# Scan stage of a hybrid encoder: inverse summed in its PSUM bank, with the early columns of two matrices as one operand

## The chip, the core and the metric

The kernel runs on one core of one Trainium2 chip. The metric is the device time of one execution in microseconds (us), as the median of several runs. TensorE (PE) multiplies matrices and writes to PSUM (eight banks of 512 float32 columns on 128 partitions), VectorE (DVE) and ScalarE (ACT) read and write both memories, GpSimd (POOL) works on SBUF, SyncE (SP) issues most of the transfers. The engines run side by side and wait for each other on semaphores; each works off its own instructions in order. All data is float32.

## What is computed

One layer: a projection feeds three mixers (gMLP, bidirectional RWKV-7, bidirectional mLSTM), their outputs are concatenated and projected, normed, and go through a mixture of 32 experts. The change is in the RWKV-7 scan. Cut from the reference:

```python
def _wkv7_step(state, inp):
    r, w, k, v, a, b = inp
    sa = jnp.einsum('phvk,phk->phv', state, a)
    state = state * w[:, :, None, :] + sa[..., None] * b[:, :, None, :] + v[..., None] * k[:, :, None, :]
    return state, jnp.einsum('phvk,phk->phv', state, r)
...
    _, out = lax.scan(_wkv7_step, state0, xs)      # 256 steps, 2 directions, 6 heads of 64
    out = _merge_dirs(...)
    out = _head_norm(out, RWKV_GN_EPS).reshape(bn, sn, R_WIDTH) * ln_g + ln_b
```

A chunk of 128 steps is done at once: with strictly triangular M (products of the vectors a and b within the chunk) the step-by-step correction is the inverse of a unit triangular 128x128 matrix. The mLSTM and expert parts are:

```python
    sc = jnp.einsum('phtd,phsd->phts', qc, kc) * jnp.exp(dmat - m_t[..., None])
...
    return ((u_ + 1.0) * (g_ * jax.nn.sigmoid(g_ * SWIGLU_ALPHA))) @ w2[e] + b2[e]
```

## The kernel before

The program is written engine by engine, each with its instructions in a fixed, hand-written order. It has three stages in time: the input projection with its preparations (to about 117 us), the scan stage (117 to 294 us), and output projection, norm, routing and experts (to the end). SP loads the experts' weights, 403 MB in all, in 2 MB loads; two of the first expert loads are issued inside the scan stage, three (L511) when the last scan output is done, and the rest follows as slots come free.

The scan stage goes over three pairs of heads (`for pt in range(NP)`), and in each pair over 2 directions d x 2 chunks x 2 heads, so that each direction has four 128x128 matrices side by side in one PSUM bank. Per pair:

- **Products.** PE multiplies keys with queries and keys with keys (L1024, contraction over 64 rows); DVE evicts each bank of 512 columns with a triangular mask (L1608) into `nqT` and `mpT`.
- **Start of the inverse.** POOL adds the identity to M (L1335) and masks off all but 2x2 blocks (L1338), giving `xmT`. PE transposes that (L1037), ACT copies it to `xm` (L733). PE also turns keys (L1032, L1033), evicted by ACT (L730).
- **Levels** m = 2, 4, 8, 16, 32, 64: the inverse of the 2m blocks comes from that of the m blocks X: PE forms M X (L1045), DVE masks the product to the blocks between an early and a late group (L1613, into `gm`), PE forms the new X (L1058, bank 4d+1) and its transpose (L1059, bank 4d+2), ACT evicts both (L738, L739). All at full width, four matrices per direction.
- **Solution, state and output.** PE and ACT work through W, U and the state in two steps over the chunks (L1087 to L1122), then ACT copies the output (L774).

Other work is woven in between the levels by hand. On PE: gate columns and bonus sums (L990, L1005), m rows (L958) and scores (L966) of the mLSTM heads, their weighing (L980), the turning of the former pair's scans (L997). On DVE after the two masks of a level: at m=2 gate rows (first pair) or `scans_out` and the first half of a norm (L1582, L1376 to L1381), and the decay scan of the next pair (L1457); at m=4 the decay arguments (L1551), the second half of the norm (L1387, L1595 to L1600), `prep_relative`; at m=8 the weights (L1561), another norm, `prep_keys`; at m=16 a norm's end, decay arguments, the division; at m=32 weights; at m=64 division and `prep_operands` (L1487 to L1492), whose end lets the next pair's products start. On ACT: roots of the norms (L691, L694), the exponentials of the factors (L725) and of the decays (L705 to L708). On POOL: the masking of the factors (L1327).

## Time and profile before

| | |
|---|---|
| median of 3 runs | 1267.39 us (1267.28 to 1267.82) |
| the profiled execution | 1271.03 us, span 1269.1 us |
| mean granted clock of TensorE | 0.993 |
| busy in the span | PE 1199.1, DVE 303.2, ACT 218.6, POOL 34.1 us |
| read from memory | 428.44 MB |
| scan stage | 117.0 to 293.7 us |

Busy times are sums over records of one engine, and a record that overlaps the next is not counted twice. A record's "idle before" is the time its engine stood still ahead of it, and the arrow names whose work ended that. PEclk is the granted clock of TensorE as a share of full speed (2.4 GHz; 0.5 is 1.2 GHz). In the chain of waits each line is a piece of the path that ended last, with start and length. A float32 matmul leaves two records each of weight load and of matmul, a transpose one. Line numbers are those of the kernel before, unless said otherwise.

### The profile page before, as it was taken

To read this page: it belongs to the slowest core of one execution; us is meant where nothing else is said; L and a number is where in the kernel's file an instruction comes from. 1 tells how busy PE (TensorE), PEld (TensorE's weight loads), DVE (VectorE), ACT (ScalarE), POOL (GpSimd) and SP (SyncE) were. 2 spreads that over 40 slices of the span, in tenths; PEclk is the share of its full clock that TensorE was granted. 3 is DMA by queue.
4 is the path that set the end of the run, shared out by engine and by line. 5 is a ranking of instruction groups with operands and counts; after the bars stand their busy time and mean duration, and the time that the engine had idled before them with its cause. 6 is when DMAs were issued, how large, how long until landed. Compare 5 with 4: busy or idle time off the path is not lost.

```text
span 1269.1 us, 15346 instructions
## 1 busy us (share of the span) xinstructions
PE 1199.1 (94%) x6265; PEld 552.5 (44%) x6265; DVE 303.2 (24%) x751; ACT 218.6 (17%) x432; POOL 34.1 (3%) x44
## 2 busy tenths in 40 slices
PE   7999999999999999999999999999999999999996
PEld 6874889795433333333333333333333333333332
DVE  1344757454511111111111111111111111111113
ACT  2233334232111111111111111111111111111112
POOL 1001020110000000000000000000000000000001
PEclk9999999999999999999999999999999999999998
DMA  9324000117999999997999999999999999999994
GB/s 334 146 88 164 1 1 1 70 69 278 371 401 429 429 428 429 428 428 301 429 430 429 428 429 429 429 427 429 429 428 429 429 428 427 430 428 429 428 428 184
DMA packets 41599, 429.89 MB, mean 339 GB/s; under 512 B 3756, under 2 KB 8851, under 8 KB 16739
## 3 DMA queue, kind: packets, MB, share of 16 engines
q1 hardware_dynamic: 39616, 426.29, 80.3%
q0 software_dynamic: 688, 2.06, 0.5%
q10 hardware_dynamic: 1267, 1.15, 0.4%
q8 instruction: 20, 0.33, 0.1%
q14 instruction: 8, 0.07, 0.0%
HBM read 428.44 MB, written 1.05 MB: 338 GB/s over the span
## 4 chain that ended last, share of the span: by engine, by line
PE 67%; DMA 21%; DVE 6%; ACT 2%; POOL 1%; issue 1%; SPq 1%; ACTq 0%; POOLq 0%; DVEq 0%
PE bank L1252 24%; DMA pool<-in_exp_w 19%; PE bank L1284 14%; PE bank L886 5%; PE bank L1226 3%; PE bank L896 3%; PE bank L1045 2%; PE bank L1059 2%; PE bank L1236 2%; PE bank L1058 2%; PE bank L1271 2%; DVE pool L1803 1%; DVE pool L1798 1%; DVE pool L1800 1%; ACT pool L823 1%
## 5 line engine op out<-in xcount | busy, mean ns | idle before, releaser
L1252 PE MATMUL bank<-pool 128*64 128x512 f32 x1024 | 230.8, 596 | 6.1 <-DMA pool<-in_exp_w 6.1
L1252 PE MATMUL bank<-ring,pool 128*64 128x512 f32 x1024 | 230.9, 596 | 5.8 <-DMA ring<-in_exp_w 5.8
L1284 PE MATMUL bank<-ring,pool 128*64 128x512 f32 x1024 | 226.8, 595 | 0.0
L1284 PEld LDWEIGHTS bank<-ring,pool 128*64 128x64 f32 x1024 | 70.7, 137 | 153.9 <-issue 153.9
L1252 PEld LDWEIGHTS bank<-pool 128*64 128x64 f32 x1024 | 70.1, 137 | 150.7 <-issue 139.1
L1252 PEld LDWEIGHTS bank<-ring,pool 128*64 128x64 f32 x1024 | 70.0, 137 | 150.7 <-issue 137.2
L1784 DVE TENSOR_SCALAR pool<-pool 128x128 f32<-128x128 f32 x64 | 19.3, 346 | 420.6 <-PE bank L1252 420.6
L1796 DVE TENSOR_SCALAR pool<-bank 128x512 f32<-128x512 f32 x32 | 22.2, 693 | 331.7 <-PE bank L1252 331.7
L1226 PE MATMUL bank<-pool 64*128 64x512 f32 x264 | 65.6, 614 | 0.7 <-ACT pool L827 0.7
L1212 PE MATMUL bank<-pool 128*64 128x512 f32 x264 | 62.3, 593 | 1.0 <-DVE pool L1757 1.0
L827 ACT ACTIVATE pool<-bank 128x512 f32<-128x512 f32 x32 | 19.1, 598 | 250.5 <-PE bank L1284 250.5
L886 PE MATMUL bank<-pool,ring 128*128 128x256 f32 x272 | 61.2, 387 | 0.0
L817 ACT ACTIVATE pool<-bank 128x256 f32<-128x256 f32 x32 | 12.3, 385 | 279.4 <-PE bank L1264 279.4
L886 PEld LDWEIGHTS bank<-pool,ring 128*128 128x128 f32 x272 | 52.6, 194 | 7.7 <-issue 0.3
L819 ACT ACTIVATE pool<-pool 128x512 f32<-128x512 f32 x32 | 20.2, 632 | 195.5 <-DVE pool L1796 195.5
L1059 PE MATMUL bank<-ring 128*128 128x128 f32 x288 | 53.5, 280 | 0.0
L1058 PE MATMUL bank<-ring 128*128 128x128 f32 x240 | 48.8, 286 | 0.5 <-DVE ring L1613 0.5
L1236 PE MATMUL bank<-pool 32*64 32x512 f32 x392 | 36.4, 610 | 9.6 <-ACT pool L823 9.6
L1059 PEld LDWEIGHTS bank<-ring 128*128 128x128 f32 x288 | 43.0, 196 | 0.2
L1226 PEld LDWEIGHTS bank<-pool 64*128 64x128 f32 x264 | 22.6, 185 | 43.2 <-issue 41.6
L1045 PE MATMUL bank<-ring 128*128 128x128 f32 x288 | 38.1, 285 | 0.8 <-ACT ring L739 0.8
L1058 PEld LDWEIGHTS bank<-ring 128*128 128x128 f32 x240 | 37.3, 196 | 2.7 <-DVE ring L1613 1.7
(295 smaller groups left out, 938.9 us busy)
## 6 DMA issues: line engine op xcount, KB each, us to landing
ring<-in_exp_w SPq DMA_DIRECT2D x127, 2048.0 KB, 20.6
pool<-in_exp_w SPq DMA_DIRECT2D x64, 2048.0 KB, 27.4
ring<-in_w_in SPq DMA_DIRECT2D x4, 2048.0 KB, 9.2
ring<-in_w_out SPq DMA_DIRECT2D x2, 2048.0 KB, 7.9
ring<-in_w_in SPq DMA_DIRECT2D x2, 1536.0 KB, 13.7
ring<-in_exp_w SPq DMA_DIRECT2D x2, 1024.0 KB, 22.3
ring<-in_w_in SPq DMA_DIRECT2D x1, 1632.0 KB, 6.4
pool<-in_consts SPq DMA_DIRECT2D x1, 1601.0 KB, 19.5
```

What stands on the lines that cost most here:

```text
L886: last = mm(bank[i % 4][:, 0:S], w[:, k, col:col + P], xT[:, k], start=(k == 0), stop=(k == KD - 1))
L896: last = mm(bank[(NT + j) % 4][:, 0:n], xT[:, k, P * c:P * c + P], w[:, k, :], start=(k == 0), stop=(k == KD - 1))
L1045: last = mm(pview(4 * d, 0, 4, P)[:, j], mpT[:, d, j, 0:P], xm[:, d, j], start=True, stop=True)
L1058: mm(pview(1 + 4 * d, 0, 4, P)[:, j], xmT[:, d, j], gm[:, d, j], start=True, stop=True)
L1059: last = mm(pview(2 + 4 * d, 0, 4, P)[:, j], gm[:, d, j], xmT[:, d, j], start=True, stop=True)
L1212: last = mm(bank[7][SLOTS * hf:SLOTS * hf + SLOTS, :], sel[:, c], x_tok[:, c, 512 * hf:512 * hf + 512], start=(c == 0), stop=(c == NCH - 1))
L1226: last = mm(bank[2 * c + hf][:, :], gT[hp, P * c:P * c + P], ysb[hp, :], start=False, stop=stop, skip_group_check=True)
L1236: last = mm(bank[4 + g][SLOTS * hf:SLOTS * hf + SLOTS, :], esel[gp], bias[gp, 512 * hf:512 * hf + 512], start=True, stop=False)
L1252: last = mm(bank[4 + g][hp, :], lhs, w[:, k % 2, o:o + 512], start=False, stop=(k == KD - 1))
L1271: last = tr(pview(4, 0, 4, P)[:, j], hr[:, j:j + 509:4], ident)
L1284: last = mm(bank[6][SLOTS * hf:SLOTS * hf + SLOTS, :], hT[:, k % 4, SLOTS * (k // 4):SLOTS * (k // 4) + SLOTS], w2s[k // 4][:, k % 4, 512 ...
L1796: V.tensor_scalar(hr, bank[4][:, :], 7.0, None, ALU.min).then_inc(s_hg, 1)
```

## The change

The levels are m = 1, 2, 4, ..., 64 now, and a level works on half the columns. Only blocks between an early group of m columns and the late group behind it change in a level. So `early_columns` (POOL) copies the early columns of M of two matrices into one 128-column operand, ACT evicts from the inverse only the late and the early columns of the next level (`y_late`, `y_early`), `cross` (PE) multiplies them, `turn_early` transposes the early columns, and `update` adds into the inverse Y, which stays in its PSUM bank (4d+1) from an identity matmul at m=1 to the end (start=False); it writes every other group of m columns there. POOL's two steps at the start of a pair, the full-width transposes and the separate transpose of X are gone. The product of b and a is formed in both orders by matmuls of 128 columns, and the key products come behind them (bank 3 and 4d+2), on PE and DVE, beside level m=1. The woven work stands at the same m as before, behind the masks of DVE. W is written to bank 4d instead of 4d+1. Constants shrink from 3202 to 2818 columns, in the same space.

```diff
-LEVELS = (2, 4, 8, 16, 32, 64)
+LEVELS = (1, 2, 4, 8, 16, 32, 64)
...
+        mp = rview(2, 2048, 2, 2, 4, P)
+        m_early = [view(o_xT + 512 * b, 2, 2, P) for b in range(4)]
+        ym = rview(3, 0, 2, 4, P)
+        tT = rview(3, 1024, 2, 2, P)
+        gm = rview(3, 2048, 2, 2, P)
...
+        def part(a, n, late):
+            return a.rearrange("p j (b two m) -> p two (j b) m", two=2, m=LEVELS[n])[:, late]
...
# ACT
+                for n in range(NL):
                     for d in range(2):
-                        if n < len(LEVELS) - 1:
-                            A(xm[:, d], pview(1 + 4 * d, 0, 4, P), ACT.Copy)
-                        A(xmT[:, d], pview(2 + 4 * d, 0, 4, P), ACT.Copy).then_inc(s_xup, 1)
+                        if n:
+                            act.wait_ge(s_tt, 12 * pt + 2 * n + d - 1)
+                            A(tT[:, d], pview(4 * d + 2, 0, 2, P), ACT.Copy).then_inc(s_tev, 1)
...
+                        if n < NL - 1:
+                            A(half_cols(y_late(d), n + 1), part(y, n + 1, 1 - d), ACT.Copy).then_inc(s_xup, 1)
+                            A(half_cols(y_early(d), n + 1), part(y, n + 1, d), ACT.Copy).then_inc(s_yup, 1)
+                        else:
+                            A(ym[:, d], y, ACT.Copy).then_inc(s_xup, 1)
...
# PE
+                def cross(n, d):
...
+                    for jj in range(2):
+                        if n:
+                            early, late = m_early[(n - 1) % 4][:, d, jj], y_late(d)[:, 2 * jj:2 * jj + 2]
+                        else:
+                            early = mp[:, d, 1, 2 * jj:2 * jj + 2].rearrange("p j s -> p (j s)")[:, d:d + 255:2]
+                            late = ident[:, 1 - d:P:2].unsqueeze(1).broadcast_to([P, 2, HD])
+                        last = mm(pview(4 * d, 0, 2, P)[:, jj], early, late, start=True, stop=True)
...
+                def update(n, d):
...
+                    for jj in range(2):
+                        lhs = tT[:, d, jj] if n else scan_const(C_T1 + P * d, P)
+                        last = mm(part(pview(4 * d + 1, 2 * P * jj, 2, P), n, 1 - d), lhs, gm[:, d, jj], start=False,
+                                  stop=(n == NL - 1), skip_group_check=True)
...
-                        for j in range(4):
-                            last = mm(pview(4 * d, 0, 4, P)[:, j], mpT[:, d, j, 0:P], xm[:, d, j], start=True, stop=True)
...
-                        for j in range(4):
-                            if n < len(LEVELS) - 1:
-                                mm(pview(1 + 4 * d, 0, 4, P)[:, j], xmT[:, d, j], gm[:, d, j], start=True, stop=True)
-                            last = mm(pview(2 + 4 * d, 0, 4, P)[:, j], gm[:, d, j], xmT[:, d, j], start=True, stop=True)
...
# POOL
-                    nc.gpsimd.tensor_tensor(m, m, ident.unsqueeze(1).broadcast_to([P, 4, P]), ALU.add).then_inc(s_pch, 1)
-                    pool.wait_ge(s_pch, 2 * pt + d + 1)
-                    x2 = scan_const(C_X2 + P * d, P)
-                    nc.gpsimd.tensor_tensor(xmT[:, d], m, x2.unsqueeze(1).broadcast_to([P, 4, P]), ALU.mult).then_inc(s_gps, 1)
+                for n in range(1, 5):
+                    early_columns(pt, n)
                 mask_factors(2 * pt)
+                for n in range(5, NL):
+                    early_columns(pt, n)
                 mask_factors(2 * pt + 1)
...
# DVE
-                        V.tensor_tensor(gm[:, d], pview(4 * d, 0, 4, P), wide(gmask(d, n), 4), ALU.mult).then_inc(s_g, 1)
+                    V.tensor_tensor(gm[:, d], pview(4 * d, 0, 2, P), wide(gmask(n), 2), ALU.mult).then_inc(s_g, 1)
```

**PE, level m=4 of the first pair.** First the kernel before, from the product of direction 0 to the first update of direction 1:

```order
L1045 MATMUL bank0<-ring 128x128 [waits x_evacuated]
L1045 MATMUL bank0<-ring 128x128 x3
L1045 MATMUL bank4<-ring 128x128 [waits x_evacuated]
L1045 MATMUL bank4<-ring 128x128 x3
L990 MATMUL bank7<-pool 128x6 [waits gate_rows_ready]
L990 MATMUL bank7<-pool 128x6 x7
L1005 MATMUL bank7<-pool 128x2 [waits bonus_products_ready]
L1005 MATMUL bank7<-pool 128x2
L958 MATMUL bank3<-ring,pool 128x256 x2
L1058 MATMUL bank1<-ring 128x128 [waits level_product_masked]
L1059 MATMUL bank2<-ring 128x128
```

The same place after the change, direction 1 of the cross products (L1083) and the transposes (L1090) up to the updates (L1100), with the changed kernel's line numbers:

```order
L1083 MATMUL bank4<-ring,pool 128x128 [waits early_columns_of_operand_ready]
L1083 MATMUL bank4<-ring,pool 128x128
L1090 MATMUL bank6<-pool,ring 128x128 [waits early_columns_of_inverse_evacuated]
L1090 MATMUL bank6<-pool,ring 128x128
L1020 MATMUL bank7<-pool 128x6 [waits gate_rows_ready]
L1020 MATMUL bank7<-pool 128x6 x7
L1035 MATMUL bank7<-pool 128x2 [waits bonus_products_ready]
L1035 MATMUL bank7<-pool 128x2
L988 MATMUL bank3<-ring,pool 128x256 [waits key_products_evacuated]
L988 MATMUL bank3<-ring,pool 128x256
L1100 MATMUL bank1<-ring 128x32x4 [waits early_columns_evacuated,level_product_masked]
L1100 MATMUL bank1<-ring 128x32x4
```

Two products and two updates stand where four and eight stood for a direction, and the update, which goes to pieces of 4 columns, waits for ACT's copy of the transposes as well as for DVE's mask.

**DVE, start of the second pair.** Before, the last four of the eight evictions and the first masks:

```order
L1608 TENSOR_TENSOR ring<-bank2,pool 128x512 [waits products_done]
L1608 TENSOR_TENSOR ring<-bank0,pool 128x512 [waits products_done]
L1608 TENSOR_TENSOR ring<-bank6,pool 128x512 [waits products_done]
L1608 TENSOR_TENSOR ring<-bank4,pool 128x512 [waits products_done]
L1613 TENSOR_TENSOR ring<-bank0,pool 128x512 [waits level_product_done]
L1613 TENSOR_TENSOR ring<-bank4,pool 128x512 [waits level_product_done]
L1582 COPY pool<-bank7 128x256 [waits scan_out_turned]
```

After, from the last of four evictions of products (L1699) on: L1693 evicts the key products, L1688 is the mask.

```order
L1699 TENSOR_TENSOR ring<-bank5,pool 128x2x2x128 [waits products_done]
L1693 TENSOR_TENSOR ring<-bank3,pool 128x512 [waits key_products_done]
L1688 TENSOR_TENSOR ring<-bank0,pool 128x256 [waits level_product_done]
L1693 TENSOR_TENSOR ring<-bank2,pool 128x512 [waits key_products_done]
L1688 TENSOR_TENSOR ring<-bank4,pool 128x256 [waits level_product_done]
L1693 TENSOR_TENSOR ring<-bank6,pool 128x512 [waits key_products_done]
L1693 TENSOR_TENSOR ring<-bank3,pool 128x512 [waits key_products_done]
L1688 TENSOR_TENSOR ring<-bank0,pool 128x256 [waits level_product_done]
L1688 TENSOR_TENSOR ring<-bank4,pool 128x256 [waits level_product_done]
L1662 COPY pool<-bank7 128x256 [waits scan_out_turned]
```

The masks of m=1 stand between the evictions of the key products, and the copy of the scans comes behind the masks of m=2, as before.

## Rows read from the trace of the kernel before

**Rows 1.** Busy times by stretch: us, PE, PEld, DVE, ACT, POOL, PEclk, DMA, GB/s.

```profile
117.03:177.46 60.43, 56.52 (x456) 50.58 (x456) 38.56 (x89) 24.31 (x52) 7.85 (x8) 0.97 0.11 36
177.46:234.65 57.19, 54.04 (x451) 48.55 (x451) 37.08 (x93) 22.38 (x51) 7.86 (x8) 1.00 0.09 32
234.65:293.74 59.09, 55.96 (x460) 50.80 (x460) 33.09 (x86) 20.46 (x47) 9.80 (x11) 0.97 0.13 45
```

**Rows 2.** Groups by shape, 119 to 296 us: count | busy us, mean ns | idle before.

```profile
L1059 PE MATMUL bank<-ring 128*128 128x128 f32 x288 | 53.5, 280 | 0.0
L1058 PE MATMUL bank<-ring 128*128 128x128 f32 x240 | 48.8, 286 | 0.5 <-DVE ring L1613 0.5
...
L1045 PE MATMUL bank<-ring 128*128 128x128 f32 x288 | 38.1, 285 | 0.8 <-ACT ring L739 0.8
...
L1327 POOL TENSOR_TENSOR pool<-pool 128x256 f32<-128x256 f32 x12 | 8.5, 727 | 94.9 <-ACT pool L725 94.9
...
L1561 DVE TENSOR_TENSOR pool<-pool,bank 128x256 f32<-128x256 f32 x12 | 5.0, 416 | 2.4 <-POOL pool L1327 2.4
...
L730 ACT ACTIVATE ring<-bank 128x256 f32<-128x256 f32 x6 | 2.3, 383 | 13.3 <-PE bank L1033 13.3
```

**Rows 3.** Chain of waits at the second pair's start: start us, us, what.

```profile
177.53 1.11 PE bank L1024 x8
...
183.93 1.27 POOL ring L1338
...
185.90 1.84 PE bank L1045 x16
```

**Rows 4.** DVE in order of time, second pair: start us, us, what [idle before].

```profile
188.39 0.42 DVE L1582 COPY pool<-bank 128x256 f32<-128x256 f32 x1
...
192.42 0.69 DVE L1613 TENSOR_TENSOR ring<-bank,pool 128x512 f32<-128x512 f32 x1
...
195.19 1.40 DVE L1551 TENSOR_SCALAR pool<-bank,pool 128x256 f32<-128x256 f32 x4 [0.64 <-PE bank L958]
...
201.10 0.69 DVE L1613 TENSOR_TENSOR ring<-bank,pool 128x512 f32<-128x512 f32 x1 [0.20 <-PE bank L1045]
...
209.22 1.52 DVE L1613 TENSOR_TENSOR ring<-bank,pool 128x512 f32<-128x512 f32 x2 [0.53 <-PE bank L1045]
...
216.06 1.52 DVE L1613 TENSOR_TENSOR ring<-bank,pool 128x512 f32<-128x512 f32 x2 [1.24 <-PE bank L1045]
...
222.92 0.69 DVE L1613 TENSOR_TENSOR ring<-bank,pool 128x512 f32<-128x512 f32 x1 [2.88 <-PE bank L1045]
```

**Rows 5.** DVE in order of time, first pair (two rows) and third pair.

```profile
134.04 1.29 DVE L1613 TENSOR_TENSOR ring<-bank,pool 128x512 f32<-128x512 f32 x2
...
151.84 1.29 DVE L1613 TENSOR_TENSOR ring<-bank,pool 128x512 f32<-128x512 f32 x2
...
257.25 0.42 DVE L1600 TENSOR_TENSOR pool<-pool 128x256 f32<-128x256 f32 x1
...
264.14 0.17 DVE L1381 TENSOR_SCALAR pool<-pool 128x4 f32<-128x4 f32 x1
```

**Rows 6.** ACT, then POOL, in order of time around m=16, second pair.

```profile
214.82 0.63 ACT L705 ACTIVATE ring<-ring 128x512 f32<-128x512 f32 x1
...
216.47 0.84 ACT L725 ACTIVATE pool<-pool 128x768 f32<-128x768 f32 x1
...
217.39 1.41 POOL L1327 TENSOR_TENSOR pool<-pool 128x256 f32<-128x256 f32 x2 [15.12 <-ACT pool L725]
```

**Rows 7.** Busy times of two stretches of 4 us, columns as in rows 1.

```profile
136.00:140.00 4.00, 4.00 (x23) 4.00 (x23) 2.60 (x9) 1.08 (x2) 0.00 (x0) 0.57 0.02 4
...
184.00:188.00 4.00, 2.75 (x23) 2.73 (x24) 0.91 (x2) 1.07 (x2) 1.19 (x1) 1.00 0.00 0
```

**Rows 8.** Chain of waits behind the scans; then the busy times of 300 us.

```profile
301.78 14.69 DMA pool<-in_ln_b
...
642.00:942.00 300.00, 291.64 (x1428) 99.44 (x1430) 38.79 (x95) 34.28 (x64) 0.00 (x0) 1.00 1.01 428
```

More of the change, by code:

```diff
@@ L62, in constants @@
         before = (row < col) if d == 0 else (row > col)
[L63 to L72 removed]
+        o = C_MASK2 + 3 * P * d
+        c[:, o:o + P] = before
+        c[:, o + P:o + 2 * P] = before | (row == col)
+        c[:, o + 2 * P:o + 3 * P] = before.T
+        c[:, C_T1 + d * P:C_T1 + d * P + P] = col == 2 * (row % HD) + d
+    for n, m in enumerate(LEVELS):
+        c[:, C_GM + n * P:C_GM + n * P + P] = (row // HD == col // HD) & (row % HD // m == col % HD // m)
     c[:, C_HSEL:C_HSEL + 2] = row // HD == np.arange(2)[None, :]
@@ L331, in encoder_kernel, with wide, rows @@
                "mg": (2 * GW + 2 * RW, RW)}
+        def wide(a, n):
+            return a.unsqueeze(1).broadcast_to([P, n] + list(a.shape[1:]))
+        def rows(key, pt):
+            o = LNO[key][0] + P * pt
+            return wide(lnb[:, o:o + P], 2)
         s_x = sem("x_loaded")
@@ L1016, in _, with key_products @@
                 pe.wait_ge(s_ops, pt + 1)
-                for n in range(0, len(FILLS), 2):
-                    d, f, _ = FILLS[n]
-                    if f == 0:
-                        pe.wait_ge(s_prev, 8 * pt + 1 + 2 * d)
+                for d in range(2):
+                    for c in range(NCH):
+                        for a in (1, 0):
+                            for h in range(2):
+                                hp = slice(HD * h, HD * h + HD)
+                                keys, queries = bt[hp, d, c], ar[hp, d, c, a]
+                                lhs, rhs = (keys, queries) if a else (queries, keys)
+                                o = 256 * c + P * (1 - a)
+                                last = mm(bank[4 * d + h][:, o:o + P], lhs, rhs, start=True, stop=True)
+                                if c == 1 and a == 0:
+                                    last.then_inc(s_prod, 1)
+                def key_products(d):
+                    if d:
+                        pe.wait_ge(s_nqe, 4 * pt + 1)
+                    elif pt:
+                        pe.wait_ge(s_oTe, pt)
                     for c in range(NCH):
@@ L1039, in _ @@
-                for n in range(len(LEVELS)):
+                                last.then_inc(s_nqf, 1)
+                def cross(n, d):
+                    if n:
+                        pe.wait_ge(s_me, 12 * pt + 2 * n + d - 1)
+                    for jj in range(2):
+                        if n:
+                            early, late = m_early[(n - 1) % 4][:, d, jj], y_late(d)[:, 2 * jj:2 * jj + 2]
[3 more added lines that the diff above has]
+                        last = mm(pview(4 * d, 0, 2, P)[:, jj], early, late, start=True, stop=True)
+                    last.then_inc(s_a, 1)
@@ L1040, in _ @@
+                key_products(0)
+                for n in range(NL):
                     for d in range(2):
-                        pe.wait_ge(s_xup, 14 * pt + 2 * n + d + 1)
                         if n == 0:
-                            pe.wait_ge(s_prev, 8 * pt + 6 + 2 * d)
-                        for j in range(4):
-                            last = mm(pview(4 * d, 0, 4, P)[:, j], mpT[:, d, j, 0:P], xm[:, d, j], start=True, stop=True)
-                        last.then_inc(s_a, 1)
-                    if n == 1:
+                            pe.wait_ge(s_prev, 4 * pt + 2 * d + 2)
+                            cross(0, d)
+                            mm(bank[4 * d + 1][:, :], ident, ident.unsqueeze(1).broadcast_to([P, 4, P]), start=True,
+                               stop=False, skip_group_check=True)
+                            continue
+                        pe.wait_ge(s_xup, 2 * NL * pt + 2 * (n - 1) + d + 1)
+                        if n == 1:
+                            pe.wait_ge(s_nqe, 4 * pt + 2 + d)
+                        if n == 2:
+                            tr(pview(4 * d + 2, 0, 4, P)[:, 2], bt[:, d, d], ident)
+                            tr(pview(4 * d + 2, 0, 4, P)[:, 3], kt[:, d, d], ident).then_inc(s_bk, 1)
+                        if n == 3:
+                            pe.wait_ge(s_bkev, 2 * pt + d + 1)
+                        cross(n, d)
+                        turn_early(n, d)
+                    if n == 0:
+                        if pt:
+                            scans_turned(pt - 1)
+                        key_products(1)
+                    if n == 2:
@@ L1314, in _ @@
         def _(pool):
+            psteps = [0]
             nc.gpsimd.memset(hst, 0.0)
@@ L1390, in flat @@
                 return a.rearrange("p c h e -> p (c h) e")
-            def rows(key, pt):
-                o = LNO[key][0] + P * pt
-                return wide(lnb[:, o:o + P], 2)
-            def wide(a, n):
-                return a.unsqueeze(1).broadcast_to([P, n] + list(a.shape[1:]))
             dve.wait_ge(s_ptr, 1)
```

183 lines of the change are left out of this document (98 added, 85 removed).

## The prediction

> **What bounds the kernel now.** I read the stretches of the three head pairs first. From the first product matmul of a pair to that of the next it takes 60.43, 57.19 and 59.09 us, 176.7 us in all, and TensorE (PE) is busy for 56.5, 54.0 and 56.0 of them, VectorE (DVE) for 38.6, 37.1 and 33.1, ScalarE (ACT) for some 22, GpSimd (POOL) for 8 to 10 [rows 1]. So the scan stage is bound by PE, and DVE is the next in line. The groups by shape say what PE does: 816 records of the level loop, L1045, L1058 and L1059 [rows 2]. One 128x128 float32 matmul leaves two records, and in the chain 16 records, 8 matmuls, take 1.84 us [rows 3]: 0.23 us a matmul. A reader on another engine starts about 0.17 us after PE could go on to the next (a record lasts 280 ns but comes every 115).
>
> Then the end of the kernel: behind the scans the expert weights stream in at 428 GB/s with the DMA share at 1.0 [rows 8], and their large loads start when the last scan output is done. The 14.69 us of the norm row behind three of these loads [rows 8] hangs on the same event. So whatever the scans save moves the stream, and with it the end, by as much. I find no cover for it.
>
> **Part 1: PE work removed.** Before, a pair has 48 + 40 + 48 = 136 matmuls of 128 columns in its levels (816/3/2) and eight transposes. Now a level from m=2 on has four products (cross), four updates and four transposes of half price (a transpose leaves one record): 8 x 0.23 + 4 x 0.11 = 2.3 us against 24 x 0.23 = 5.5. Six such levels are 13.7 us, the new level m=1 with its two 512-column identity matmuls (four times 128 columns each, 0.9 us) is 3.6. Sum 17.3 against 136 x 0.23 + 0.9 = 32.2: 15 us of PE work per pair, 45 in all. PE then needs about 40 us per pair. That is no longer far from DVE's 37, and neither engine will be busy all the time, so the sum must be made along the path.
>
> **Part 2: DVE.** The eight evictions of 512 columns per pair stay. Twelve masks of 512 columns at 0.69 us become fourteen of 256. The nearest row for such a mask is L1561, 0.42 us with one operand in PSUM [rows 2]. The norm steps, decay arguments, weights and preparations stay where they were, between the masks, and there they are the bound from now on.
>
> **Part 3: the start of a pair.** Before, DVE's evictions, two POOL steps for each direction (1.27 us each, the last at 183.93), the transposes and an ACT copy stand in series: first product 177.5, first level product 185.9, the first pair of masks done and the next DVE block started at 188.39, 10.9 us in [rows 3, 4]. After: PE's own row is 1.8 (products) + 0.95 (key products) + 2 x (0.45 + 0.9) (cross and identity) + 0.4 (turning the last pair's scans) + 0.95 (other key products) + 0.45 (first update) = 7.3; then 0.17, an ACT copy of 256 columns (L730: 0.38, [rows 2]), a cross of 0.45 and 0.17 again put the first m=2 mask at 8.5, the second 0.7 later, the block at 9.5. POOL's copies of early columns are not in it: priced as L1327, 0.73 us for 128x256 [rows 2], eight of them from 2.5 us on end at 8.5, and level n needs only the n-th two. If such a copy cost 1.3 as the older POOL steps do, the third level's would still be in time.
>
> **Part 4: the levels, worked for the second pair.** Times from its first product, now | then:
> - m=2 block (scan output, norm, decay scan) 188.39 to 192.42 [rows 4]: 4.0 us of pure DVE, unchanged. Masks m=4 at 15.0 | 13.5.
> - m=4: before, DVE waited until 195.19 for the m rows behind 12 updates and products, then worked 5.9 us to the next mask at 201.10. Now the m rows are ready by 13.7; two masks and a copy take 0.9, the rest 5.7. Masks m=8 at 23.6 | 20.1.
> - m=8: 8.12 us now (201.10 to 209.22), PE-bound by little. Two masks at 0.34 plus 6.1 of weights, norm and key preparation: 6.8. Masks m=16 at 31.8 | 26.9.
> - m=16: 6.84 now. Masks and 4.2 of DVE work: 5.0. Masks m=32 at 38.6 | 31.9.
> - m=32: 6.86 now (216.06 to 222.92). Then: the chain here is not DVE. The decay arguments are out at 30.2; ACT copies the m=16 results until 29.3, runs the decay exponentials (1.65, from 214.82 to 216.47) and then the factors (0.84) until 31.7; POOL masks them (1.41) until 33.1 [rows 6], DVE multiplies until 34.4, PE weighs (1.3) until 35.7 and only then issues the cross for m=64, whose mask starts at 36.3 | 45.5 before.
> - m=64 and the tail: the rest of the level is 1.7 us of PE; from the last update to the next pair's first product it is 9.1 now and stays, since its steps only change banks (the last mask starts at 222.92, it and the 16 records of its updates take 2.6, and 225.5 to 234.65 is the 9.1).
> Sum: 36.3 + 1.7 + 9.1 = 47.1 against 57.2, a gain of **10.1**.
>
> **First pair.** Its m=2 block is 2 us longer (gate rows; next masks at 134.04) and the m=8 block 1.1 us longer, ending at 151.84 [rows 5]; the start is 0.4 shorter, and at m=8 the factors' masking on POOL is waited for. The same walk gives 48.0 against 60.4: **12.4**, of which 1.7 is a stretch at half clock that the trace has at 136 to 140 [rows 7].
> **Third pair.** No preparation for a fourth: its blocks end at 257.67 (L1600) and 264.3 (L1381) [rows 5], 1.4, 1.7 and 2.9 us shorter than the second's. Today PE covers that; then it is gained, with PE bound in the last levels. The walk gives 43.5 against 59.1: **15.6**.
> Sum 38.1 us.
>
> **The clock.** In 136 to 140 the granted clock was 0.57, about 1.2 GHz for most of it, and PE worked on [rows 7]; the third pair, at a mean of 0.97 [rows 1], must hold another. In the first pair PE had waited shortly before, for the gate rows. In the new kernel PE waits more often: by my walk some 5 us nearly idle before m=32 in the first two pairs and 2 us at m=4. I allow for two to three such stretches on the path, 1.7 us each: 4 us. The Trainium skill ("TensorE: Matmul & The Clock Gate", What's actually happening) says that the throttled clock is the default and that activity releases it; the trace agrees as far as it goes, and by that rule alone every idle level start would be a candidate.
> Forecast gain 38 - 4 = **34 us**. The profiled execution took 1271.0 us around a span of 1269.1, 3.6 above the median 1267.4 of the runs; it would go to 1237, the median to **1233.4**.
>
> **A rule against the change.** The update writes its result into every other group of m columns of a PSUM bank. No row shows a matmul that does this: all level rows write 128 columns in a row at 0.23 us [rows 2, 3]. Bounds: no extra, or twice the time, as if each column took a second cycle. Doubling adds 0.9 us to each level's PE work; it stays hidden in the DVE-bound levels m=4 to m=16 and shows at m=1, 2, 32 and 64: about 3.5 us per pair, 10 us in all, 1244. The Trainium skill ("SBUF — State Buffer", Door 1: The DMA port swizzle) states that non-contiguous PSUM access significantly slows matmuls; it gives no factor. I take none, since from m=2 on the columns come in runs and only m=1 writes single ones, and keep 10 us for the range.
>
> **Rivals.**
> - *Slow PSUM writes*, as priced: 1240 to 1247. Chance 0.10.
> - *Half clock over much of the scans*: one more us for each us of PE work so run. With a third of the 120 us, two thirds of them on the path less the waits: 15 to 25 us back, 1245 to 1260. For it: the stretches there are. Against: PE at 2.75 busy of 4 us at 184 to 188 kept its full clock there and in the second pair after it [rows 1, 7]. Chance 0.07.
> - *Slower than before*: the same mechanism without end. If nearly all of the new scans' 120 us of PE work ran at 1.2 GHz, 120 comes on top of 139, less some 18 of waits: 240 against 177, 1330. It decides from about 55 us of PE work at half clock. Chance 0.02.
> - *DVE and POOL hold each other up, or the chain through ACT copies is longer than rows show* (nine ACT copies and exponentials per level with two hand-overs each): 2 to 4 us per pair, 1238 to 1245. Chance 0.11.
> - *The gain does not reach the end*, because the weight stream is bound by an earlier start: it would stay at 1267 with DMA waits growing. The DMA share of 0.09 to 0.13 in the scans [rows 1] speaks against it. Chance 0.02.
> - *More than forecast*: no half-clock stretch and overlaps that I put in series: 1222 to 1228. Chance 0.10.
> - The forecast, 1228 to 1240: 0.58.
>
> **How the numbers follow.** Faster by more than 0.2% (2.5 us, about what can be told from no change): all but the fifth and the slower one, 0.95. Same 0.02, slower 0.03. Range: 1224 to 1249, which leaves out the tails of the clock cases and of the better one, near 0.18.
>
> **What would show it.** In the new profile: three pairs of about 47, 48 and 43 us; PE busy near 40 in each; 256-column masks near 0.42; after them no DVE wait at m=8 and m=16; update records as quick as the cross ones (else the PSUM rival); the granted clock by stretch; the time from the last scan output to the end unchanged at 975 us. Wrong if a pair stays above 52 us, or if that last stretch grows.

## The result, and the profile after

| | before | after |
|---|---|---|
| median, runs of one chip | 1267.61 us (1267.28 to 1268.63, 4 runs) | 1250.24 us (1246.84 to 1253.96, 4 runs) |
| ratio | | 0.9862 (95%: 0.9831 to 0.9894) |
| profiled execution | 1271.03 us, span 1269.1 | 1248.53 us, span 1246.7 |
| mean granted clock | 0.993 | 0.979 |

Faster, by 17.4 us instead of the 34 forecast; 1250.2 lies one microsecond outside the range. The kernel after also scatters: its four runs took 1246.84, 1248.53, 1251.96 and 1253.96 us at mean granted clocks of 0.984, 0.979, 0.978 and 0.976, in that order.

The three pairs in the kernel after, as [rows 1] are before (columns: us, then PE, PEld, DVE, ACT and POOL busy, PEclk, DMA share, GB/s):

```profile
115.22:170.79 55.57, 49.03 (x333) 41.02 (x333) 36.10 (x91) 24.24 (x66) 7.07 (x16) 0.82 0.11 39
170.79:223.39 52.60, 46.30 (x328) 38.80 (x327) 35.40 (x95) 22.28 (x65) 8.18 (x16) 0.87 0.09 33
223.39:270.63 47.24, 44.30 (x337) 37.67 (x337) 31.73 (x88) 20.47 (x61) 9.64 (x19) 0.93 0.16 58
```

155.4 us instead of 176.7 before and 138.6 forecast. The records of PE fell from 1367 to 998, but it is busy for 139.6 us and not for the 120 of the forecast, because the granted clock is 0.82, 0.87 and 0.93 where it was 0.97, 1.00 and 0.97 [rows 1]. From the last scan output (270.63) to the end of the span it takes 976.1 us, against 975.4 before: what the scans save arrives at the end, as forecast.

PE in order of time in the second pair, around the update of m=8 (L1100), the weighing (L1010), the m rows (L988) and the cross products of m=16 (L1083):

```profile
187.93 0.71 PE L1083 MATMUL bank<-ring,pool 128*128 128x128 f32 x4
...
189.14 0.38 PE L1090 MATMUL bank<-pool,ring 128*128 128x128 f32 x2
192.75 2.07 PE L1100 MATMUL bank<-ring 128*128 128x128 f32 x8 [3.23 <-DVE ring L1688]
194.62 2.66 PE L1010 MATMUL bank<-pool 128*128 128x65 f32 x12
197.21 2.07 PE L988 MATMUL bank<-ring,pool 6*128 6x256 f32 x4
199.21 1.22 PE L1083 MATMUL bank<-ring,pool 128*128 128x128 f32 x4
```

And the busy times of the stretches of 4 us there:

```profile
188.00:192.00 4.00, 1.52 (x12) 1.28 (x12) 3.83 (x9) 1.41 (x4) 3.82 (x6) 0.97 0.00 0
192.00:196.00 4.00, 3.25 (x15) 3.25 (x16) 3.86 (x12) 1.32 (x4) 0.00 (x0) 0.50 0.00 0
196.00:200.00 4.00, 4.00 (x13) 3.04 (x14) 2.91 (x7) 0.42 (x2) 0.00 (x0) 0.50 0.00 0
200.00:204.00 4.00, 3.27 (x19) 2.91 (x17) 2.61 (x8) 2.00 (x7) 0.00 (x0) 0.75 0.00 0
204.00:208.00 4.00, 3.21 (x12) 2.51 (x13) 2.51 (x11) 2.57 (x7) 1.41 (x2) 0.68 0.00 0
```

PE waits 3.23 us for DVE's m=8 masks, the clock goes to 0.50, that is 1.2 GHz, and the work behind the wait takes 1.7 to 1.8 times as long as the same records do at full clock (in e1_fill below): the update 2.07 us against 1.16, the weighing 2.66 against 1.55, four cross records 1.22 against 0.71. In turn DVE waits for PE, and of the 10.1 us forecast for this pair 4.6 arrive. Over the whole stage such stretches add up to 41 us at half clock; before they were 7. (In every figure of this kind a 4-us window with a granted clock of c counts as 2 x (1 - c) x 4 us at half clock, and the windows are summed.)

### The profile page after: what moved, and what is told of

Same layout as the page of the kernel before. It is cut to its first block, busy times and chain, and to the rows that moved or that the text cites. A ratio compares the mean times of both kernels' runs of the same rounds, so it can differ in the third digit from the quotient of the medians.

```text
span 1246.7 us, 14734 instructions
## 1 busy us (share of the span) xinstructions
PE 1172.2 (94%) x5893; PEld 519.7 (42%) x5893; DVE 297.7 (24%) x757; ACT 218.4 (18%) x474; POOL 33.5 (3%) x68
## 4 chain that ended last, share of the span: by engine, by line
PE 67%; DMA 20%; DVE 7%; ACT 2%; issue 1%; SPq 1%; ACTq 0%; POOL 0%; POOLq 0%; DVEq 0%
PE bank L1326 24%; DMA pool<-in_exp_w 20%; PE bank L1358 15%; PE bank L916 5%; PE bank L1300 3%; PE bank L926 3%; PE bank L1310 2%; PE bank L1211 2%; PE bank L1083 2%; PE bank L1345 2%; DVE pool L1899 1%; DVE pool L1894 1%; PE bank L1100 1%; DVE pool L1896 1%; ACT pool L853 1%
## 5 line engine op out<-in xcount | busy, mean ns | idle before, releaser
L1326 PEld LDWEIGHTS bank<-pool 128*64 128x64 f32 x1024 | 70.3, 137 | 151.0 <-issue 138.4
L1345 PE MATMUL bank<-pool 128*128 128x128 f32 x128 | 24.0, 310 | 15.3 <-DVE pool L1899 15.3
L1345 PEld LDWEIGHTS bank<-pool 128*128 128x128 f32 x128 | 17.9, 209 | 43.4 <-DVE pool L1899 43.4
L926 PE MATMUL bank<-ring,pool 128*128 128x384 f32 (+2 forms) x96 | 35.3, 528 | 0.0
L1286 PEld LDWEIGHTS bank<-pool 128*64 128x64 f32 x264 | 18.9, 137 | 38.2 <-issue 37.1
L1100 PE MATMUL bank<-ring 128*128 128x128 f32 x144 | 27.0, 331 | 6.1 <-DVE ring L1688 5.7
```

The costliest lines, as they stand in the source:

```text
L926: last = mm(bank[(NT + j) % 4][:, 0:n], xT[:, k, P * c:P * c + P], w[:, k, :], start=(k == 0), stop=(k == KD - 1))
L1100: last = mm(part(pview(4 * d + 1, 2 * P * jj, 2, P), n, 1 - d), lhs, gm[:, d, jj], start=False, stop=(n == NL - 1), skip_group_check=True)
L1286: last = mm(bank[7][SLOTS * hf:SLOTS * hf + SLOTS, :], sel[:, c], x_tok[:, c, 512 * hf:512 * hf + 512], start=(c == 0), stop=(c == NCH - 1))
L1326: last = mm(bank[4 + g][hp, :], lhs, w[:, k % 2, o:o + 512], start=False, stop=(k == KD - 1))
L1345: last = tr(pview(4, 0, 4, P)[:, j], hr[:, j:j + 509:4], ident)
```

## Experiments

Theory: PE, with a good quarter less to do (998 records instead of 1367), waits for DVE more often; the clock falls at such waits; the PE work behind them is on the path. Rivals: the path at full clock is simply longer than I walked it (DVE and POOL hold each other up, long hand-overs through ACT), or the updates' strided PSUM writes are slow.

### Filling PE's waits

```diff
+fill_sum(SUM_FILL[pt][n])        # k x mm(bank[1][:, 0:P], zeros, ident, start=False, stop=False)
 for d in range(2):
     update(n, d)
+fill_cross(CROSS_FILL[pt][n])    # k x mm(bank[0][:, 0:P], ident, ident, start=True, stop=True)
+SUM_FILL:   8 ahead of the gate columns; m=8: 8, 12, 5; m=16: 10, 6, 2 (pairs 1, 2, 3)
+CROSS_FILL: m=4: 2, 2, 2; m=16: 6, 6, 7
```

The fillers need a matrix of zeros, so 128 columns of constants are loaded more; the other variants with fillers have them too.

> The changed kernel, with 76 matmuls of 128x128 put into TensorE's waits: 51 of zeros, summed into the inverse's own bank before the updates (no value changes), 25 whose result nobody reads, in the cross bank, before the scores. At 0.23 us each that is 17.5 us of matmuls in places where PE waits 16 to 20 us for VectorE. Theory (the clock falls to 1.2 GHz after the waits, and what PE does next at half speed is on the path): the 4-us stretches of the scans with a granted clock near 0.5, 41 us of them in the changed kernel, go but for a few us; the pairs take 48 to 51, 48 to 50 and 43 to 46 us instead of 55.6, 52.6 and 47.2; the time 1234 to 1239 us, ratio to before 0.974 to 0.978, and the runs lie within 2 us of each other. Rival A (the path at full clock is longer than I walked it: held-up VectorE, long ACT chain): the clock is mended, but the time stays at 1247 to 1252. Rival B (filler work is only more work): 1252 to 1262.

Measured: 1238.72 us (1237.80 to 1239.09), ratio 0.9736 (0.9720 to 0.9752), mean clock 0.995. On this chip before took 1270.53. The three pairs:

```profile
117.29:167.00 49.71, 48.10 (x401) 41.53 (x401) 36.12 (x91) 24.12 (x66) 7.33 (x16) 1.00 0.13 44
167.00:216.00 49.00, 46.52 (x380) 39.61 (x379) 35.39 (x95) 22.07 (x65) 8.20 (x16) 1.00 0.10 37
216.00:262.07 46.07, 44.80 (x369) 38.41 (x369) 31.63 (x88) 20.27 (x61) 9.65 (x19) 1.00 0.17 58
```

No stretch at half clock is left and the pairs take 144.8 us, 10.6 less than in the changed kernel, although PE has 76 matmuls more. The numbers of the theory came in, the narrow scatter too; only the third pair, at 46.07 us, lies a shade above its 43 to 46. Rival B is out, and so is rival A as the whole cause. In part rival A holds: at full clock the pairs still take 6.2 us more than the 138.6 forecast.

The same kernel decides on the PSUM rival, since its clock is 1.00 throughout. Groups by shape of the three pairs (count | busy us, mean ns | idle before); L1086 are the cross products, L1103 the updates:

```profile
L1086 PE MATMUL bank<-ring,pool 128*128 128x128 f32 x144 | 23.3, 285 | 0.1
L1103 PE MATMUL bank<-ring 128*128 128x128 f32 x144 | 22.3, 288 | 1.0 <-DVE ring L1704 1.0
...
L1103 PE MATMUL bank<-ring,pool 128*128 128x128 f32 x24 | 3.5, 288 | 0.0
```

The updates, which write every other group of m columns of a bank, take 288 ns a record, the cross products, which write their columns in a row, 285. The last row is the updates of m=1, where single columns are written: 288 as well. There the chain of waits of the kernel after has four updates in the time of any four products (start us, us, what):

```profile
177.85 1.09 PE bank L1100 x8
```

So for float32 writes of this kind the statement of the Trainium skill that I had kept a range for ("SBUF — State Buffer", Door 1) shows no effect here.

### The same instructions with six columns

```diff
-mm(bank[1][:, 0:P], zeros, ident[:, 0:P], ...)
+mm(bank[1][:, 0:6], zeros, ident[:, 0:6], ...)      (the cross fillers likewise)
```

> As e1_fill with the same 76 instructions in the same places, but each with 6 columns instead of 128, so PE is hardly busier. Theory: that they are there changes nothing; the clock stays at half in the same stretches, 1247 to 1254 us as the changed kernel. Rival (it is the issuing or the order that helps, not the columns): the time follows e1_fill.

Measured: 1256.41 us (1252.62 to 1269.56, 10 runs), ratio 0.9912 (0.9877 to 0.9947). The first two pairs, and then one filler group (24 records, 12 matmuls) at full clock and one of 12 records at half:

```profile
115.89:172.12 56.23, 55.34 (x401) 48.11 (x401) 36.09 (x91) 24.16 (x66) 7.06 (x16) 0.85 0.11 39
172.12:229.40 57.28, 56.20 (x379) 49.25 (x379) 35.37 (x95) 22.27 (x65) 8.17 (x16) 0.79 0.09 31
```

```profile
192.29 2.74 PE L1110 MATMUL bank<-pool 128*128 128x6 f32 x24
...
203.34 2.56 PE L1110 MATMUL bank<-pool 128*128 128x6 f32 x12
```

The clock falls as without fillers (47.8 us at half clock), so their mere presence does nothing. The median lies 2.4 us above the 1247 to 1254 expected, and the runs form two groups, six at 1252.6 to 1256.6 us and four at 1266.1 to 1269.6; why is open. In one thing the expectation was wrong: PE is not "hardly busier". A 6-column matmul with 128 x 128 weights takes the 0.23 us of a 128-column one. By the rows PE is busy for 55.3 of 56.2 us and yet runs at 0.85; with 128 columns in the same places it is busy for less and runs at 1.00. A full PE row in the profile is no proof of a kept clock.

### The kernel after again, and one pair filled

> The changed kernel once more, unaltered, as the partner of the other runs on the same chip: ratio to before near 0.986 (0.983 to 0.989), with the 5 to 8 us of spread that its half-clock stretches give it.

Measured, on one chip with the next two and e8: 1253.31 us (1247.89 to 1253.65), ratio 0.9842 (0.9811 to 0.9872). Its profiled run has 47.8 us at half clock and 159.8 us of scans.

```diff
-SUM_FILL, CROSS_FILL of e1_fill for all pairs
+the same for pair 2 alone
```

> The changed kernel with filler matmuls in the second pair alone: 18 of zeros before the updates of m=8 and m=16, 8 before the two scores. Theory (each wait is followed by its own stretch of half clock, whose price is paid there): the second pair shrinks from 52.6 to 49 us and its slices from 192 to 212 us show the clock at 1.0; the first and third keep their stretches and 55 to 56 and 47 us; 3 to 4 us below the unaltered kernel. Rival (the clock of the whole scan stage hangs together, or fillers give back what they save): the second pair stays at 52 or more, or the third gets shorter as well.

Measured: 1245.40 us (1243.12 to 1247.91), ratio 0.9798 (0.9771 to 0.9826).

```profile
116.97:172.53 55.56, 49.00 (x333) 41.08 (x333) 36.11 (x91) 24.25 (x66) 7.08 (x16) 0.82 0.11 39
172.53:221.55 49.02, 46.52 (x380) 39.60 (x379) 35.42 (x95) 22.10 (x65) 8.22 (x16) 1.00 0.11 36
221.55:267.62 46.07, 43.25 (x337) 36.24 (x337) 31.64 (x88) 20.42 (x61) 9.67 (x19) 0.96 0.17 59
```

The first pair is that of the changed kernel (55.57, and 55.53 in e5), the second that of e1_fill: the waits of the second pair pay their price there. The third pair did get shorter without fillers, as the rival said: 46.07 us against 47.24 and, in e5 on this chip, 50.30. It has 3.4 us at half clock where they have 6.8 and 10.2, so of the 7.9 us between the medians (3 to 4 were expected) only a part belongs to the fillers, and the two intervals of the ratio overlap. Whether the second pair's fillers had a hand in the third is open, since this pair varies in the unfilled kernel too. That it took as long as the filled third pair of e1_fill says that 3.4 us at half clock cost no more there than 16 fillers.

### Half the fillers, and fillers in the wrong place

```diff
-SUM_FILL, CROSS_FILL of e1_fill
+each number halved (37 matmuls)
```

> e1_fill with half as many filler matmuls in each place (37 instead of 76). Theory as far as it goes says nothing on how full the waits must be. If busy time counts in proportion, half of the 10 to 12 us come back: 1243 to 1247, 0.979 to 0.982. If a wait cut to 1 or 2 us is enough to keep the clock, as e1_fill, 0.974; if half filled is as good as not filled, as the changed kernel, 0.985.

Measured: 1244.42 us (1241.56 to 1247.08), ratio 0.9785 (0.9760 to 0.9809): half way. 20.5 us at half clock are left, and the pairs take 54.25, 49.00 and 46.08 us: the first loses 4.5 us against e1_fill for 14 us at half clock, the second, which has 13 fillers fewer than there, nothing for 7 us. I take it that a stretch of half clock costs something only where PE's work is the path; no run shows this by itself.

```diff
-SUM_FILL, CROSS_FILL of e1_fill
+m=2: 13, m=64: 12 ahead of the updates, in each pair
```

> The changed kernel with 75 filler matmuls, as many as in e1_fill, in places where PE does not wait: 13 before each update of m=1's successor m=2 and 12 before each of m=64, all three pairs. Theory (it is the waits before m=8, m=16 and the scores that count, not the amount of PE work in the stage): the half-clock stretches stay, some 40 us of them, and the 17 us of fillers lie on the path: 1262 to 1270 us, 0.995 to 1.001. Rival (the mean activity of the stage sets the clock): the half clock goes and pays for the fillers, 1246 to 1254.

Measured: 1264.27 us (1259.54 to 1265.51), ratio 0.9927 (0.9902 to 0.9951), 37.5 us at half clock. 75 matmuls that fill no wait leave the half clock where it was and lie on the path: 169.1 us of scans, 9 to 14 more than the kernel after. The time fell into the range expected, the ratio just below its 0.995. What matters is where the work stands, not how much of it the stage has; and by e2_tiny not each kind of work will do.

### What POOL does to DVE

In the block after the m=4 masks three products of DVE take 0.84, 0.83 and 0.50 us, where they were 0.43 each before. DVE in order of time, second pair of the kernel after, then POOL:

```profile
188.10 0.84 DVE L1677 TENSOR_TENSOR pool<-pool 128x256 f32<-128x256 f32 x1
188.98 0.83 DVE L1679 TENSOR_TENSOR pool<-pool 128x256 f32<-128x256 f32 x1
189.84 0.50 DVE L1680 TENSOR_TENSOR pool<-pool 128x256 f32<-128x256 f32 x1
```

```profile
187.93 1.59 POOL L1402 TENSOR_TENSOR pool<-pool 128x256 f32<-128x256 f32 x2 [10.93 <-ACT pool L752]
189.48 2.35 POOL L1420 COPY pool<-ring 128x256 f32<-128x256 f32 x4
```

I first took the copies (L1420) away from there.

```diff
-m_early = [view(o_xT + 512 * b, 2, 2, P) for b in range(4)]
+m_early = [... four as before] + [rview(3, o, 2, 2, P) for o in (1536, 2560)]
-for n in range(1, 5): early_columns(pt, n)
+for n in range(1, NL): early_columns(pt, n)
 mask_factors(2 * pt)
-for n in range(5, NL): early_columns(pt, n)
```

> The changed kernel with POOL's copies of the early columns of all six levels made before the first factor mask, in six buffers instead of four, so that none runs beside VectorE's m=4 block. Theory (POOL's copies there lengthen VectorE's steps, 1.2 us in the second pair): 1 us less per pair where the block is the path, 1246 to 1249 us; the steps that took 0.84, 0.83 and 0.50 us are back at 0.43. Rival (no effect of POOL on VectorE; something else made these steps long): they stay at 0.8, and the time at 1250. If the clock alone decides, the time can go either way by 3 us.

Measured: 1246.47 us (1245.58 to 1250.42), ratio 0.9797 (0.9781 to 0.9813). The time came in by luck, for the step expected failed: two of the three products still took 0.84 and 0.83 us, and only the last went to 0.42. The second pair is 0.8 us shorter, the first as long as in the kernel after (55.57), the third 0.6 longer: 155.3 us in all against 155.4, both with 41.0 us at half clock. That the median is 6 us better than e5_after's ratio would give is not shown to be the copies' work; the mean clock differs from run to run, 0.979 to 0.988 here and 0.977 to 0.981 in e5_after.

The same edit on top of e1_fill:

> e1_fill and e3_early6 together. If both theories hold and add up: 2 to 3 us below e1_fill, 1231 to 1237 us, near the 1233.4 forecast. If VectorE's block is no longer the path once PE waits are filled: as e1_fill.

Measured: 1240.07 us (1237.69 to 1244.25), ratio 0.9753 (0.9725 to 0.9781), not different from e1_fill. The second pair took 48.57 instead of 49.00, the third 47.58 instead of 46.07, with 3.4 us at half clock that had come back at 236 to 244. It missed the 2 to 3 us expected.

The products that were left long stood beside the factor masks (L1402), so these were held back.

```diff
+if pt:
+    pool.wait_ge(s_rel if pt + 1 < NP else s_grp, 3)
 mask_factors(2 * pt)
```

> e1_fill with POOL's first factor mask of the second and third pair held back until VectorE has finished its norm steps and decay preparation. In e3_early6 the copies were gone from there and two of VectorE's all-SBUF products still took 0.84 and 0.83 us instead of 0.43; only the third went from 0.50 to 0.43. So the theory now: POOL's two masks (1.6 us there, 1.41 elsewhere) run against them. Expect 0.43 for all three, POOL's masks back at 1.41, 0.9 us less in each of pairs 2 and 3, 1.5 to 2 us below e1_fill's 0.9736, that is 0.972 to 0.973. Rival (the steps are long for their own sake, since other operations write or read these tiles): they stay at 0.84.

Measured: 1239.10 us (1238.65 to 1242.36), ratio 0.9743 (0.9722 to 0.9764), not different from e1_fill. The same three products, and POOL's masks, line numbers 16 or 18 higher:

```profile
183.76 0.43 DVE L1695 TENSOR_TENSOR pool<-pool 128x256 f32<-128x256 f32 x1
184.22 0.43 DVE L1697 TENSOR_TENSOR pool<-pool 128x256 f32<-128x256 f32 x1
184.68 0.43 DVE L1698 TENSOR_TENSOR pool<-pool 128x256 f32<-128x256 f32 x1
```

```profile
186.86 1.42 POOL L1418 TENSOR_TENSOR pool<-pool 128x256 f32<-128x256 f32 x2 [14.21 <-DVE ring L1564]
```

The mechanism is shown: DVE products with both operands in SBUF take twice as long beside a POOL product, and POOL's grow from 1.42 to 1.59. The Trainium skill ("SBUF — State Buffer", Who interferes with whom) has it as a rule: a DVE instruction with two SBUF inputs contends with a POOL instruction that reads SBUF. The trace agrees. But the gain did not come. The m=8 masks started 20.3 us into the second pair instead of 21.5, and then DVE stood still for 0.92 us ahead of the weights, which need the factor masks that now come late (POOL ends them at 188.28, the weights start at 188.37); the pair took 48.78 us instead of 49.00. In the third pair 6.8 us at half clock appeared at 236 to 248 and it took 49.27. Why the clock fell there in e4 and e7 and not in e1 is open: in e4 PE had no wait above 0.23 us in the 11 us before.

### Taking the waits away instead

```diff
 n == 2 (m=4):   -rwkv_norm_b(pt - 1)
 n == 3 (m=8):   -prep_keys(pt + 1)
 n == 6 (m=64):  +prep_keys(pt + 1) ahead of prep_operands, +rwkv_norm_b(pt - 1) last
```

The counts that two waits of DVE stand for were adapted to the new order.

> The changed kernel without any filler; instead VectorE's work is moved out of the blocks that PE waits for: the 3.6 us of norm steps of the last pair's scans from the m=4 block, and the 2.6 us of key preparation from the m=8 block, both to behind the last mask (m=64), where VectorE idles for some 8 us. Theory (PE's waits before m=8 and m=16 are what lengthens the scans and also what lowers the clock): PE's wait of 3.2 us before the m=8 update goes; at an unchanged clock 9 to 11 us less in the three pairs, and fewer half-clock stretches on top: 1236 to 1242 us, 0.975 to 0.980. Rival A (the clock falls as before, at other waits): 1240 to 1246. Rival B (the path is ACT and PE, not VectorE's blocks): 1248 to 1252.

Measured: 1243.81 us (1241.60 to 1246.99), ratio 0.9785 (0.9756 to 0.9813), pairs of 52.0, 46.9 and 51.2 us. The time misses the 1236 to 1242 of the theory and lies in rival A's range: 34.2 us at half clock are left, behind other waits. The wait of 3.2 us is gone and the second pair shorter than any filled one. The third grew: PE stands still for ACT, and ACT for the tail's norm, that the moved steps hold up on DVE (PE, then ACT, in order of time):

```profile
259.15 1.97 PE L1173 MATMUL bank<-pool,ring 128*128 128x64 f32 x8 [2.29 <-ACT pool L789]
```

```profile
258.35 0.21 ACT L718 ACTIVATE pool<-pool 128x4 f32<-128x4 f32 x1 [2.43 <-DVE pool L1468]
```

```diff
 n == 4 (m=16):  args(2 * pt + 1) ahead of the norm instead of behind it
 n == 5 (m=32):  +rwkv_norm_b(pt - 1) behind the weights, third pair alone
 n == 6 (m=64):  rwkv_norm_b(pt - 1) in the second pair alone
```

> e8_move with its two faults mended, and no filler: in the third pair the norm steps of the last scans come right after the weights at m=32, so that they no longer stand ahead of the tail's norm, on which ACT and then PE waited 2.3 us in e8_move; and at m=16 VectorE computes the decay arguments before the normalization instead of after it, which takes away PE's wait of 1.6 us (2.4 in the first pair) before the scores. Left is the wait of 1.9 us for the gate rows in the first pair. Theory (the clock falls where PE waits for VectorE): the half-clock stretches of pairs 2 and 3 go, those of pair 1 stay in part; pairs of 49 to 51, 45 to 46.5 and 43 to 45 us; 1230 to 1236 us, 0.969 to 0.973. Rival A (moving alone shortens the path, the clock falls anyway): 1237 to 1242, 0.974 to 0.978. Rival B (the moved work comes to lie on the path elsewhere): as e8_move or longer, 0.978 and up.

Measured: 1235.70 us (1233.06 to 1237.01), ratio 0.9718 (0.9701 to 0.9735), as expected but for the second pair, which came out shorter than its 45 to 46.5:

```profile
117.22:167.48 50.26, 45.56 (x333) 37.93 (x333) 36.37 (x91) 24.13 (x66) 7.11 (x16) 0.90 0.13 43
167.48:212.09 44.61, 40.85 (x328) 33.76 (x327) 34.65 (x95) 21.96 (x65) 7.48 (x16) 1.00 0.05 12
212.09:256.37 44.28, 41.62 (x337) 34.87 (x337) 30.42 (x88) 20.16 (x61) 9.02 (x19) 1.00 0.24 89
```

With no filler at all pairs 2 and 3 keep the full clock; 10.2 us at half clock are left, all in pair 1 at 132 to 144, behind the 1.86 us that PE waits for the gate rows at 131.67. The work of DVE is the same, it only lies where nobody waits for it.

```diff
+fill_sum(8) ahead of the gate columns of the first pair
+CROSS_FILL: m=4: 2, m=16: 2, in each pair
```

> e9_reorder with 20 filler matmuls of 128x128: eight before the gate columns of the first pair, two before each of the six scores. Theory: the first pair's half clock goes too: granted clock 0.99 or more, 2 to 4 us below e9_reorder, and runs within 2 us of each other. Rival (what half clock e9 keeps has other causes): as e9_reorder, or up to 1.5 us slower by the fillers.

Measured: 1230.54 us (1230.08 to 1236.43), ratio 0.9688 (0.9658 to 0.9717). The first pair falls to 46.83 us and no half clock is left in the scans of the profiled run; the pairs take 135.7 us. One run of four took 1236.43 at a clock of 0.990, so "within 2 us" was missed by that one. The 5.2 us below e9_reorder are more than the 2 to 4 expected, and the two intervals of the ratio just overlap; what the profile shows for the fillers are the 3.4 us of the first pair. Against e1_fill, also at full clock, the pairs are 9.1 us shorter (135.7 against 144.8): so much of moving DVE's work is path, not clock. This version, the change with DVE's work reordered and 20 filler matmuls, beats both kernels: 40.5 us less than before on the same chip, where the kernel after gains 17 to 20.

## Why the prediction failed, point by point

| us | before | forecast | after | e1_fill (full clock) |
|---|---|---|---|---|
| pair 1 | 60.43 | 48.0 | 55.57 | 49.71 |
| pair 2 | 57.19 | 47.1 | 52.60 | 49.00 |
| pair 3 | 59.09 | 43.5 | 47.24 | 46.07 |
| sum | 176.7 | 138.6 | 155.4 | 144.8 |

- **The failed step is the clock's term.** I had seen a half-clock stretch in [rows 7], counted the waits, and allowed 4 us for "two to three such stretches on the path, 1.7 us each". There were 41 us at half clock, in all three pairs, and they cost 10.6 us in the profiled execution (155.4 - 144.8) and 15.0 in that of e5. I listed 5 us of waits before m=32 and 2 us at m=4, but not that PE would stand still 3.2 us before the m=8 update (2.3 in the first pair), and that its work behind such a wait is the path. Two pairs stayed above the 52 us that I had named as the sign of being wrong. The rival "half clock over much of the scans", which I gave 0.07, is what happened, at a smaller size: it reckoned with 40 us of PE work at half clock, and 41 us of time are some 20 us of work. That two thirds of the extra time lie on the path was about right: 41, 47.8 and 10.2 us at half clock are at most 20.5, 23.9 and 5.1 us of extra time (an estimate that takes PE as busy throughout), and 10.6, 15.0 and 3.4 us of it (the last between e9 and e10) reached the end of the scans, 0.52 to 0.67.
- **A misreading under it.** I wrote that before the stretch of [rows 7] "PE had waited shortly before, for the gate rows". It had not (kernel before, PE in order of time; L990 are the gate columns):

```profile
132.23 1.16 PE L1045 MATMUL bank<-ring 128*128 128x128 f32 x8 [0.28 <-ACT ring L739]
133.32 0.66 PE L990 MATMUL bank<-pool 6*128 6x6 f32 x8
133.91 0.61 PE L1005 MATMUL bank<-pool 128*128 128x2 f32 x4
134.45 1.13 PE L958 MATMUL bank<-ring,pool 6*128 6x256 f32 x4
```

  The only wait here is 0.28 us. What stood ahead of this stretch was not a wait but work on few rows or few columns; whether that brought the fall is not shown. So counting waits could not give the whole of the clock's term, though the fillers (e1, e12) show that waits decide most of it in the new kernel.
- **The path at full clock** was forecast 6.2 us short. (e1_fill's 76 fillers are in it; with half of them pairs 2 and 3 took 49.00 and 46.08 us, so they add next to nothing there.) This is the rival "DVE and POOL hold each other up, or the chain through ACT copies is longer than rows show", to which I gave 0.11, at the lower end of its 2 to 4 us per pair. In the second pair DVE's first masks of each level stand so in e1_fill (DVE in order of time, first product at 167.00):

```profile
175.92 0.42 DVE L1704 TENSOR_TENSOR ring<-bank,pool 128x256 f32<-128x256 f32 x1 [0.55 <-PE bank L1086]
...
180.89 0.75 DVE L1704 TENSOR_TENSOR ring<-bank,pool 128x256 f32<-128x256 f32 x2
...
188.50 0.74 DVE L1704 TENSOR_TENSOR ring<-bank,pool 128x256 f32<-128x256 f32 x2
...
195.28 0.75 DVE L1704 TENSOR_TENSOR ring<-bank,pool 128x256 f32<-128x256 f32 x2
...
200.53 0.42 DVE L1704 TENSOR_TENSOR ring<-bank,pool 128x256 f32<-128x256 f32 x1 [0.41 <-PE bank L1086]
...
204.97 0.42 DVE L1704 TENSOR_TENSOR ring<-bank,pool 128x256 f32<-128x256 f32 x1 [2.14 <-PE bank L1086]
```

  From first product: 8.9, 13.9, 21.5, 28.3, 33.5 and 38.0 us, forecast 8.5, 13.5, 20.1, 26.9, 31.9 and 36.3. Step by step the walk was right within 0.3 us (5.0, 6.8, 5.3 and 4.4 against 5.0, 6.8, 5.0 and 4.4) but for one: m=4 to m=8 took 7.6 instead of 6.6, and 1.2 us go when POOL is held back (e7), though only 0.2 of them reach the end of the pair. Before, POOL's factor masks ran at 200.85, after DVE's norm products at 197.9 to 199.2; in the new kernel PE delivers earlier, and they meet. In the third pair I also left out the eight records of the gMLP mixing in the tail (1.06 us). The rest of the 6.2 us was not traced.
- **Parts 1 and 2** held: 256-column masks take 0.42 us (forecast 0.42), POOL's copies 0.41 alone and not 0.73, and PE at full clock needs 139.4 us with 76 fillers of 0.23 us, so about 122, forecast 120. **Slow PSUM writes** are refuted.
- **The end** held: 976.1 against 975.4 us behind the last output. The rival that the gain does not reach it is refuted.
- **The sum.** Forecast for the profiled execution was 1237, measured 1248.5: 6.2 (path), 6.6 (clock beyond 4) and 0.7 (tail), less 1.8 (and 0.2 of rounding), as the scans began at 115.22 and not at 117.03. This start is no gain of the change: the same kernel in e5 has 117.04, the other variants 116.7 to 117.3 and one 115.9. For the profiled execution it is luck: without it this would lie further from the forecast. To the medians another 5.3 come: I took the profiled run to lie 3.6 above the median as before, and it lay 1.7 below.

## What to carry to other kernels

When a change takes work from the engine that bounds a stage, forecast its waits and its clock as carefully as its work: for each new wait of TensorE ask what it does next and whether that is on the path. Mend such waits first by moving the other engine's work that nobody waits for behind the last hand-over (e9: 0.9718 from 0.9842, without a single new instruction), and fill what is left with matmuls as wide as the kernel's own (e10, and e1 against e2). And whatever becomes earlier meets new neighbours: look for pairs of DVE and POOL instructions that read SBUF side by side.

## What the runs showed of the hardware that I had not expected

- Behind waits of 1.4 to 3.4 us in between busy stretches the clock fell to 1.2 GHz, and it stayed there for 3 to 20 us, through stretches in which PE was busy all the time (196 to 200 above: 4.00 of 4.00). The Trainium skill ("TensorE: Matmul & The Clock Gate", HAM oscillation) describes this for a kernel that waits for DMA in each round, and advises to reorder the loop; here the wait is for VectorE, and reordering helped likewise (e9).
- A wait is neither always followed by a fall nor always needed for one. With waits of 1.54 us at 152.98 in e9 and 1.52 at 149.22 in e10 the clock stayed at 1.00. In the kernel before at 136, in the kernel after at 240 and in e4 at 239 it fell behind PE work with no wait above 0.40 us in the 6 us before. What decides in these cases is open.
- The same kernel draws differently from run to run: 41.0 us at half clock in one profiled execution and 47.8 in another, 1246.8 to 1254.0 us. With full clock four runs lay within 1.3 us (e1).
- A float32 matmul of 6 columns with 128 x 128 weights takes 0.23 us, as long as one of 128 columns, and leaves PE shown as busy; with 76 of them in its waits the clock fell all the same (e2), with 128 columns it did not (e1).
- float32 PSUM writes to single columns at a stride of two cost nothing extra: 1.09 us for four matmuls, 288 ns a record against 285.
